# A trunk of attention and experts: expert rows gathered and scattered as half rows over all partitions

## What is computed

```python
def moe_ffn(h, w_router, router_bias, wg, wu, wd):
    b, s, d = h.shape
    t = h.reshape(b * s, d)
    scores = jax.nn.sigmoid((t @ w_router).astype(jnp.float32))
    ...
    _, idx = lax.top_k(jnp.where(in_group, sel, -jnp.inf), TOP_K)
    gate = jnp.take_along_axis(scores, idx, axis=-1)
    gate = gate / jnp.sum(gate, axis=-1, keepdims=True)
    combine = jnp.sum(jax.nn.one_hot(idx, N_EXPERTS, dtype=jnp.float32) * gate[..., None], axis=1)
    hg = jnp.einsum('nd,edf->nef', t, wg)
    hu = jnp.einsum('nd,edf->nef', t, wu)
    act = jax.nn.silu(hg) * hu * combine[:, :, None].astype(t.dtype)
    out = jnp.einsum('nef,efd->nd', act, wd)
    return out.reshape(b, s, d)

for l in range(DEPTH):          # DEPTH = 2
    ...                         # attention, x = x + mixed @ w_out[l]
    x = x + moe_ffn(rms_norm(x, ffn_norm[l]), w_router, router_bias, w_gate[l], w_up[l], w_down[l])
```

## Time and profile before

| | us |
|---|---|
| median of 3 runs (1990.13 to 1992.47) | 1991.15 |
| profiled execution | 1984.46 |
| its span, first to last instruction | 1982.7 |
| PE busy | 1869.7 (94%) |
| DVE busy | 1587.1 (80%) |
| ACT busy | 1431.7 (72%) |
| POOL busy | 86.2 (4%) |
| DMA, hardware queue, share of 16 engines | 70.3% |
| DMA, software queue | 5.7% |
| mean granted TensorE clock | 0.972 |

### The profile page before, as it was taken

The page is one execution under the profiler, slowest core; times in us unless marked ns, Lnnn a source line. Parts: engine busy times, 40 slices in busy tenths (PEclk is TensorE's granted clock), DMA queues, the critical chain, the costliest instruction groups (busy, mean ns, idle before and its releaser), DMA issues.

```text
span 1982.7 us, 30643 instructions
## 1 busy us (share of the span) xinstructions
PE 1869.7 (94%) x9018; PEld 1507.4 (76%) x9018; DVE 1587.1 (80%) x2242; ACT 1431.7 (72%) x2279; POOL 86.2 (4%) x86
## 2 busy tenths in 40 slices
PE   7999999997999998989999999999889999998998
PEld 6887888886777777767778878888767777777775
DVE  5566777657999999989975667765689999998998
ACT  5465665446899888888755556664569988888895
POOL 0000000001000000000000000000010000000000
PEclk9999999997999999999999999999879999999999
DMA  7554444566999999999866444445579999999997
GB/s 276 200 187 150 149 165 156 192 226 224 399 404 414 404 404 405 405 387 418 336 221 232 149 170 154 166 149 203 211 269 397 410 406 417 408 404 394 393 422 265
DMA packets 82860, 582.08 MB, mean 294 GB/s; under 512 B 11662, under 2 KB 11918, under 8 KB 13166
## 3 DMA queue, kind: packets, MB, share of 16 engines
q1 hardware_dynamic: 75600, 542.01, 70.3%
q0 software_dynamic: 7168, 38.94, 5.7%
HBM read 575.91 MB, written 29.36 MB: 305 GB/s over the span
## 4 chain that ended last, share of the span: by engine, by line
PE 60%; DMA 16%; issue 8%; DVE 7%; ACT 7%; ACTq 0%; DVEq 0%; SPq 0%; POOL 0%; POOLq 0%
PE bank L867 11%; PE bank L869 11%; PE bank L868 11%; DMA raw<-in_expert_units 8%; DMA proj<-in_expert_units 7%; PE bank L1023 4%; PE bank L1025 4%; PE bank L1042 3%; PE bank L1044 3%; PE bank L1043 3%; ACT wh L582 2%; DVE wl L1223 2%; PE bank L1014 2%; DVE xl L1223 1%; PE bank L1006 1%
## 5 line engine op out<-in xcount | busy, mean ns | idle before, releaser
L1215 DVE TENSOR_TENSOR wl<-raw,wh 128x1024 fp32r<-128x1024 f32 x256 | 310.1, 1222 | 226.7 <-ACT wh L573 226.5
L573 ACT ACTIVATE wh<-raw 128x1024 fp32r<-128x1024 f32 x256 | 269.0, 1056 | 265.0 <-PE bank L869 262.8
L867 PE MATMUL bank<-wh,xh 128*128 128x512 f32 x1024 | 415.5, 406 | 2.3 <-DVE wl L1215 2.1
L869 PE MATMUL bank<-wh,xl 128*128 128x512 f32 x1024 | 401.9, 393 | 0.0
L868 PE MATMUL bank<-wl,xh 128*128 128x512 f32 x1024 | 400.6, 391 | 0.0
L1223 DVE TENSOR_TENSOR wl<-proj,wh 128x1024 fp32r<-128x1024 f32 x256 | 302.8, 1219 | 32.6 <-ACT wh L582 31.9
L1223 DVE TENSOR_TENSOR wl<-raw,wh 128x1024 fp32r<-128x1024 f32 x256 | 302.6, 1219 | 26.2 <-ACT wh L582 25.6
L582 ACT ACTIVATE wh<-proj 128x1024 fp32r<-128x1024 f32 x256 | 261.1, 1051 | 51.3 <-PE bank L1044 21.8
L582 ACT ACTIVATE wh<-raw 128x1024 fp32r<-128x1024 f32 x256 | 261.0, 1052 | 47.0 <-PE bank L1044 20.9
L1023 PE MATMUL bank<-wh,xh 128*128 128x512 f32 x648 | 271.0, 418 | 4.5 <-DVE xh L1664 3.0
L1025 PE MATMUL bank<-wl,xh 128*128 128x512 f32 x648 | 262.3, 405 | 0.0
(11 more groups left out here) (259 smaller groups left out, 2717.6 us busy)
## 6 DMA issues: line engine op xcount, KB each, us to landing
raw<-in_expert_units SPq DMA_DIRECT2D x192, 1024.0 KB, 15.8
proj<-in_expert_units SPq DMA_DIRECT2D x192, 1024.0 KB, 15.9
raw<-in_in_units SPq DMA_DIRECT2D x96, 1024.0 KB, 4.9
raw<-in_out_units SPq DMA_DIRECT2D x32, 1024.0 KB, 4.8
expert_rows<-rows POOLq DMA_DIRECT2D x4, 1024.0 KB, 4.5
proj<-picks POOLq DMA_DIRECT2D x4, 1024.0 KB, 7.8
x<-in_x SPq DMA_DIRECT2D x2, 1024.0 KB, 6.8
wide<-in_norms POOLq DMA_DIRECT2D x2, 1024.0 KB, 5.1
```

The source lines that it names most:

```text
L573: act_(wh[:, h % CUT, :], ring[j][:, h % 2 * HALF:(h % 2 + 1) * HALF], ACT.Copy)\
L867: mm(out, xh[:, at, tok], rh, start=start, stop=False)
L869: return mm(out, xl[:, at, tok], rh, start=False, stop=stop)
L1215: v.tensor_tensor(wl[:, h % CUT, :], ring[(first + h // 2) % slots][:, h % 2 * HALF:(h % 2 + 1) * HALF], wh[:, h % CUT, :].bitcast(F32), A ...
```

## The change

The rows in memory are seen as twice as many half rows of 1024. A gather has 128 indices: partitions 0 to 63 take the left halves of the 64 slots, partitions 64 to 127 the right halves. The turning takes square blocks, 128x128, eight per expert; each block holds the same 128 columns of the left and of the right half, so a bank has blocks of (column block, side, slot), and the two moves out of PSUM read it in the order (side, column block, slot). The output is stored as two halves in the two halves of the partitions, and scattered with 128 indices. The token table holds doubled numbers less `NOWHERE`, so that adding `NOWHERE + side` to what the matmul gives makes a valid index for a used slot and one out of bounds for an unused one (zero); the compare and the chain behind it go. The last joined rows move from `rows[:, 0]` to `rows[:, 1]`, and the two expert outputs share `rows[:, 0]`.

```diff
-    put("token", np.arange(P)[:, None] + P * np.arange(NT)[None, :] + 1)
+    put("token", 2 * (np.arange(P)[:, None] + P * np.arange(NT)[None, :]) - NOWHERE)
...
-        gathered = [spare[0:SLOTS, (4 + b) * D:(5 + b) * D] for b in range(2)]
-        picked = [spare[:, 4 * D:5 * D], spare[:, 5 * D:6 * D], rows[:, 1, :], wide[:, :]]
-        last_rows = rows[SLOTS:STACK, 0, :]
+        gathered = [spare[:, 4 * D + b * HALF:4 * D + (b + 1) * HALF] for b in range(2)]
+        picked = [spare[:, 4 * D:5 * D], spare[:, 5 * D:6 * D], rows[:, 0, :], wide[:, :]]
+        last_rows = rows[SLOTS:STACK, 1, :]
...
-        expert_out = [rows[0:SLOTS, b, :] for b in range(2)]
+        expert_out = [rows[:, 0, b * HALF:(b + 1) * HALF] for b in range(2)]
...
+        def chunks(b, g):
+
+            return stacked[b].rearrange("p (h c) n -> p h c n", h=2)[:, :, 4 * g:4 * g + 4, :]
+
+        def turned_pair(m):
+
+            return bank[m][:, :].rearrange("p (c h n) -> p h c n", h=2, n=SLOTS)
...
-                    e.indirect_dma_start(gathered[k % 2], None, rows_dram[:, :],
-                                         bass.IndirectOffsetOnAxis(ap=tok_at[0:SLOTS, k % NE, :], axis=0),
-                                         bounds_check=SEQ - 1, oob_is_err=False)\
+                    e.indirect_dma_start(gathered[k % 2], None, rows_dram.rearrange("r (h n) -> (r h) n", h=2),
+                                         bass.IndirectOffsetOnAxis(ap=tok_at[:, k % NE, :], axis=0),
+                                         bounds_check=2 * SEQ - 1, oob_is_err=False)\
...
-                    e.indirect_dma_start(picks_dram[:, :],
-                                         bass.IndirectOffsetOnAxis(ap=put_at[0:SLOTS, k, :], axis=0),
+                    e.indirect_dma_start(picks_dram.rearrange("r (h n) -> (r h) n", h=2),
+                                         bass.IndirectOffsetOnAxis(ap=put_at[:, k, :], axis=0),
                                          expert_out[k % 2], None,
-                                         bounds_check=2 * SEQ - 1, oob_is_err=False)\
+                                         bounds_check=4 * SEQ - 1, oob_is_err=False)\
...
-                    act_(stacked[b][:, 8 * g:8 * g + 8, 0:SLOTS],
-                         bank[m][:, :].rearrange("p (c n) -> p c n", n=SLOTS), ACT.Copy).then_inc(S["xt_hi"], 1)
+                    act_(chunks(b, g)[:, :, :, 0:SLOTS], turned_pair(m), ACT.Copy).then_inc(S["xt_hi"], 1)
...
-                    ins = act_(expert_out[b][:, k * COLS:(k + 1) * COLS], bank[2 + k][0:SLOTS, :], ACT.Copy,
+                    side = slice(k // 2 * SLOTS, (k // 2 + 1) * SLOTS)
+                    to = rows[0:SLOTS, 1, k * COLS:(k + 1) * COLS] if joined else \
+                        expert_out[b][side, k % 2 * COLS:(k % 2 + 1) * COLS]
+                    ins = act_(to, bank[2 + k][0:SLOTS, :], ACT.Copy,
...
-                for c in range(8):
-                    at = (8 * g + c) * P
-                    last = e.transpose(bank[m][:, c * SLOTS:(c + 1) * SLOTS], gathered[b][:, at:at + P],
-                                       ident[0:SLOTS, 0:SLOTS])
+                for c in range(4):
+                    at = (4 * g + c) * P
+                    last = e.transpose(bank[m][:, c * P:(c + 1) * P], gathered[b][:, at:at + P], ident)
...
-                    v.tensor_tensor(stacked[b][:, k, SLOTS:STACK], bank[m][:, :].rearrange("p (c n) -> p c n", n=SLOTS),
-                                    stacked[b][:, k, 0:SLOTS].bitcast(F32), ALU.subtract).then_inc(S["xt_lo"], 1)
+                    v.tensor_tensor(chunks(b, g)[:, :, :, SLOTS:STACK], turned_pair(m),
+                                    chunks(b, g)[:, :, :, 0:SLOTS].bitcast(F32), ALU.subtract)\
+                        .then_inc(S["xt_lo"], 1)
...
-                    v.tensor_scalar(pick[s, 0, a:b], slots[s, a:b, 0], 0.0, NOWHERE, ALU.is_equal, ALU.mult)\
-                        .then_inc(S["dve_done"], 1)
-                    e.wait_ge(S["dve_done"], t_.due("dve_done"))
...
+                    v.tensor_copy(slots[0:SLOTS, a:b, :], found)
+                    for side in range(2):
+                        s = slice(side * SLOTS, (side + 1) * SLOTS)
...
+                        v.tensor_scalar(put_at[s, a:c, 0], found[:, 0:c - a, 1], NOWHERE + side, None, ALU.add)
+                        ins = v.tensor_scalar(tok_at[s, a:c, 0], found[:, 0:c - a, 0], NOWHERE + side, None, ALU.add)
```

More of the change, by code:

```diff
@@ L847, in _ @@
                     for k in range(4):
-                        store(0, k, NE - 2)
+                        store(0, k, NE - 2, joined=True)
                     for k in range(4):
@@ L1070, in join @@
                         last = mm(bank[JOIN_BANK[j] + t][:, :], back[t],
-                                  rows[:, 0, j * COLS:(j + 1) * COLS], start=True, stop=True)
+                                  rows[:, 1, j * COLS:(j + 1) * COLS], start=True, stop=True)
                     last.then_inc(S["joined"], 1)
@@ L1692, in tables @@
                     e.wait_ge(S["slot_banked"], t_.due("slot_banked"))
[L1693 to L1707 removed]
+                    found = bank[2 if b <= FIRST else 4][0:SLOTS, 4 * a:4 * b].rearrange("p (n k) -> p n k", k=4)
+                    c = min(b, LAST)
+                    v.tensor_copy(slots[0:SLOTS, a:b, :], found)
+                    for side in range(2):
+                        s = slice(side * SLOTS, (side + 1) * SLOTS)
+                        if b == NE:
+                            v.tensor_scalar(tok_at[s, LAST:NE, 0], found[:, LAST - a:NE - a, 0], NOWHERE + side,
+                                            2.0 * SEQ - 1.0, ALU.add, ALU.min)
+                        v.tensor_scalar(put_at[s, a:c, 0], found[:, 0:c - a, 1], NOWHERE + side, None, ALU.add)
+                        ins = v.tensor_scalar(tok_at[s, a:c, 0], found[:, 0:c - a, 0], NOWHERE + side, None, ALU.add)
                     ins.then_inc(S["tables_ready"], 1)
```

16 lines of the change are left out of this document (2 added, 14 removed).

## The result

The changed kernel takes **1954.05 us** (median of 4 runs, 1949.59 to 1956.39) against 1990.64 us for the kernel before in the same comparison (4 runs, 1979.19 to 1992.47): a ratio of 0.9821, 95% interval 0.9803 to 0.9840. The forecast was 1962, the range 1953 to 1985. The profiled execution of after took 1956.39 us (span 1954.2), that of before 1984.46 (span 1982.7): 28.1 us less, where the medians are 36.6 us apart.

A forecast was written before the change was run, and what follows sets the result against it. The prediction took the DMA to bound the expert parts once the weight ring ran dry. Holes 31.3 us less 2 for pieces gave 29.3 of gain, from a median of 1991.15 to 1962 us, range 1953 to 1985.

The forecast's parts named there:

- The bound: Expert part of each layer: engines set the pace until the ring of eight weight units runs dry, then the DMA.
- Holes, 31.3 us: DMA rate drops after gathers into 64 partitions; gathering over all 128 removes them, about 1.1 us for each of 28.
- The two ends of that cost: Gather holes: all 31.3 us goes if half the partitions cause them, nothing if reading by index does; the first was taken.
- Pieces, -2 us: Gathers and scatters with 128 indices make 3840 more packets, costing 2 us, between 0 and 7.
- GpSimd and the layer's start, 0: Doubled indices may double GpSimd's instruction time, but idle time and gather 0's 2.3 us cover hide it: 0, bounds -1 to +2.
- the sign of trouble: At layer 1's start, a first turn later than 468.4 or PE waiting for gather 0 means its cover is gone.
- Square turns and the moves' new shape, 0: Four 128x128 turns for eight save PE 0.1 us twice per expert; reshaped PSUM moves cost nothing; 0 in the sum.
- Sum and median: A gain of 29.3 us takes the profiled run from 1984.46 to 1955.2 us and the median from 1991.15 to 1962.
- Holes stay: Rival: reading by index makes the gathers' holes, so they remain; 1993 us, no change; chance 0.10.
- Half stay: Rival: one end of the gather transfer is mended, the other was part of the cost; 1977 us; chance 0.08.
- Engine bound: Rival: the new shape doubles VectorE's two moves, raising a step's floor to 31.93 us; 1985 us; chance 0.04.
- Bunching: Rival: pieces of 24 rows use 6 of 16 DMA engines, 1.1 us more per transfer; 2024 us, slower; chance 0.08.

The follow-up runs named there:

- plain copies: Each gather replaced by an unindexed copy of the first 64 rows: into partitions 0 to 63 on the kernel before, 2007.82 us; over all on the changed kernel, 1959.52 us.
- Gather alone: Changed kernel, but output stored and scattered as 64 whole rows as before; 1954.37 us, ratio 0.9823.
- void indices: Kernel before, whole rows still gathered into partitions 0 to 63, but with 128 indices, the upper 64 void; 1974.90 us, ratio 0.9923.
- half rows into 0 to 63: Kernel before, each gather replaced by two plain copies of 64 half rows (4 KB pieces) into partitions 0 to 63; 2009.47 us.
- scatter alone: Kernel before, but output stored and scattered as half rows over all partitions, gathers unchanged; 1987.43 us, ratio 0.9992.
- each gather twice over 128 partitions: Changed kernel with 24 extra unused gathers of 128 half rows over all partitions, each behind a regular gather; 1980.62 us.

## Why the prediction was right, by its steps

**The bound.** Right. First the engines at 30.5 us a step, then the DMA; what the DMA saved came out at the end, 16.0 us in layer 1, 17.8 in layer 2. The waits for it fell to 7.6 and 11.8 us where "a few" was said, since the DMA is still the bound of the later steps.

**Holes, 31.3 us.** The mechanism, a destination in half of the partitions, was right in the main, as the plain copies show; that a third of the cost goes by how the transfer is laid out, with the destination unchanged, was not in it. The size was a little small. Gather alone gave 1021.86 - 987.41 = 34.5 us in the expert parts, as much as the 34.2 that the mean of the window had offered before anything was subtracted. Two things were left out of the 31.3. The window 500 to 900 us begins after gathers 2 and 3. And the dips at the start of the row 1480 to 1580, which I subtracted as not the gathers' own (1.8 us), shrank too. The same stretch after the first gather, 1469 to 1569 us after:

```profile
GB/s 397 419 403 374 406 426 436 429 426 413 429 419 416 419 419 420 419 419 419 423 423 410 416 416 419 423 423 433 420 423 419 423 426 408 421 423 423 423 423 413
```

(24 + 2 + 18 + 47 + 15) x 2.5 / 421 = 0.6 us, so 1.2 of 1.8 went. The dip at 510 to 515 us of layer 1 stayed, as assumed.

**The two ends of that cost** were a scatter from 64 partitions without a hole, and the reload over all partitions. Choosing them over "read by index" was right: the plain copy has no index and has the holes.

**Pieces, -2 us.** Not needed. The expert parts of gather only (987.4 us, 1792 packets fewer) and of the changed kernel (988.1 and 986.1) are alike, and the software queue's share fell. The prediction suspected that this queue's surplus over the hardware queue contained the holes. That is not borne out: with void indices the share is 5.2%, while two thirds of the time are still lost.

**GpSimd and the layer's start, 0.** Right. A gather's instruction takes 2.0 us on average for 1.5, up to 2.6, and a scatter's 1.00 for 0.94; behind a gather GpSimd still idles 13 us. Gather 0 lands 4.2 us after its issue, as before, and the first turn is at the same place, right behind the last slot list:

```profile
468.54 0.67 PE L1070 MATMUL bank<-const,wide 128*128 128x128 f32 x2
468.78 1.30 PEld L1016 LDWEIGHTS bank<-const,proj 128*128 128x128 f32 x6
469.00 1.27 PE L1016 MATMUL bank<-const,proj 128*128 128x128 f32 x5
```

469.00 is later than the 468.4 named as the sign of trouble, but the whole execution was 0.7 us later by then (first gather at 462.67 for 461.93), and PE waits for no gather.

**Square turns and the moves' new shape, 0.** Right on the sum. By line, all 64 moves of each engine:

```profile
L1672 DVE TENSOR_TENSOR xh<-bank,xh 128x512 fp32r<-128x512 f32 x64 | 43.6, 681 | 1.7 <-ACT xh L775 1.7
...
L775 ACT ACTIVATE xh<-bank 128x512 fp32r<-128x512 f32 x64 | 37.1, 580 | 17.6 <-PE bank L1016 17.6
```

681 ns where the earlier trace rows has 683, and 580 for ScalarE where all 64 moves before took 581 on average. The floor of a step fell by 0.1 us, to 30.46, for the 0.2 said, but these are two effects: with the new gather and the old store it fell by 0.37 us, to 30.19, and the store in halves, which the prediction had put at nothing, took 0.27 back. In the sum neither shows, as the expert parts of the two kernels are alike.

**Sum and median.** 1984.46 - 29.3 = 1955.2 was forecast for the profiled execution, 1956.39 came: 33.8 us in the expert parts where 29.3 were counted, less 4.4 in the attention part that nobody had counted. Two misses of nearly the same size cancelled, and that is luck.

The medians tell more. Their gain is 1990.64 - 1954.05 = 36.6 us (31.9 to 39.2 by the interval), and 36.3 when measured again, where 29.3 were forecast; the first lies 1.1 us inside the range, the second just outside. What was mis-sized is the term of the holes with its deduction for pieces: 31.3 - 2, where the expert parts gave 33.8. The other 2.8 us can't be placed, because the one profiled execution of before was unusually short: all other executions of that kernel on record but two (1979.19 and 1980.15) took longer than its 1984.46 us. Carrying the gain over to the median was sound, and doing it by ratio gives the same 1962; 1955.2, the forecast for the profiled execution, lies near the measured median only because too small a gain was taken from too short a run.

**Rivals.** Holes stay: excluded. Half stay: not here, though the void indices show a transfer that keeps two thirds of its cost, by another mechanism than the one named. Engine bound: the new shape costs nothing. Bunching: no hole after scatters beyond the small dips above, and a scatter in halves alone changed nothing. Its price in the prediction was also too high: it took the 6 engines of 24 rows with the bytes of 32, which by the same dealing would use 8 and lose 0.6 us, not 1.1.

## What to carry over

Where DMA is the bound, look at its rate in slices shorter than one transfer takes to land: here a transfer into half of SBUF hid in a busy share of 9 out of 10 and a mean 4% too low, and it took time from the other queue's traffic. Lay even small side transfers over both halves of the partitions within one transfer; two transfers, one for each half, didn't help. And check a forecast gain against the difference of the medians: one profiled execution on each side was 8 us off it here (28.1 for 36.6), and made a gain that was sized too small look exact.

## What the runs showed of the hardware beyond that

**The attention part of layer 2 took longer, at a lower clock.** The attention part of layer 2, which no kernel here edits, takes 469.5 us in the kernel before and 467.8 to 470.1 in five others whose expert parts have the deep holes; it takes 472.6 to 474.2 in all seven whose holes are gone or shallower. One run with holes, half rows into 0 to 63, has 473.1 and is an exception. The granted clock says where. These are single profiled executions, one for each kernel and two for the changed one. Windows of 20 us beginning 20 and 180 us after the load of the picks, before, then after (columns as above):

```profile
992.00:1012.00 20.00, 16.50 (x80) 13.12 (x80) 18.53 (x30) 13.18 (x24) 0.00 (x0) 0.91 0.79 295
1152.00:1172.00 20.00, 20.00 (x96) 16.45 (x95) 12.30 (x30) 11.61 (x39) 0.00 (x0) 1.00 0.42 155
```

```profile
977.00:997.00 20.00, 16.98 (x72) 12.64 (x71) 17.72 (x29) 11.46 (x22) 0.00 (x0) 0.83 0.73 274
1137.00:1157.00 20.00, 19.22 (x84) 15.36 (x85) 11.04 (x18) 10.34 (x35) 0.00 (x0) 0.91 0.50 176
```

TensorE is granted 0.83 for 0.91 and 0.91 for 1.00, a mean between its levels of 1.2 and 2.4 GHz, so (0.08 + 0.09) x 20 = 3.4 us of full clock are lost, most of the 4.4. Up to 440 us after the load of the picks, the other windows of 20 us read 1.00 in both. In the second window the clock is 0.83 to 0.91 in all eight kernels with the long attention part, the exception among them (0.91 in the first, 0.84 in the second), and 1.00 in the other six. It doesn't order the six: the scatter alone has 1.00 in both windows and still takes 470.1 us.

What makes the clock fall is open. Before it, in the expert part, TensorE was busy 94.7% of the time (468.59 of 495 us) against 93.8% (478.38 of 510). But the run with each gather twice over 128 partitions was busy 93.2% of its expert part (471.42 of 505.67 us), less than before, and took 474.2 us, so how busy it was does not by itself explain the clock. Nor is it shown that this lowers the gain of the change: the medians differ by 36.6 us, more than the 33.8 of the expert parts, and the time before the first gather varies by as much from run to run (459.1 to 463.8 us).

**A store of half rows slows the engines' pace only with the new gather.** The first steps take 30.46 us in the changed kernel, 30.19 with its gather alone (scatters from 534.53 to 655.28, four steps), 30.57 with the scatter alone and 30.56 before. It costs nothing that can be measured, since the DMA sets the later steps; why the store matters in one and not in the other wasn't tried.
